# Half 0 of a norm ahead of half 1, attention scores on 64x64 tiles, mLSTM's norm and Hyena's convolution on three engines

## The chip, the cores and the metric

One Trainium2 chip, one of its cores. The metric is the device time of one execution in microseconds. The engines are TensorE (PE, with its weight loads PEld), VectorE (DVE), ScalarE (ACT), GpSimd (POOL) and SyncE (SP), each with its own instruction queue; they wait for each other by semaphores. DMAs are issued from queues of SyncE, Pool and ScalarE.

## The reference

Two transformer blocks on x of 1 x 1024 tokens x 1024 channels, all in float32. The first has a gated linear recurrence (HGRN2) beside a windowed attention; the second has four mixers of 256 channels each beside one another. Both end with a gated FFN of 2816 hidden channels. The parts that the change touches:

```python
def rms_norm(x, g): ...                    # x * rsqrt(mean(x*x) + eps) * g, ahead of each block's projections and FFN, and last
def neighborhood_attention(u, rpb):        # 4 heads of 64, rows of 64 tokens, 8 rows of keys for each row of queries
    s = jnp.einsum('bhrqd,bhrkud->bhrqku', qb, kb) * scale + bias
    p = jax.nn.softmax(s.reshape(s.shape[:4] + (kh * NA_KSPAN,)), axis=-1)
    return jnp.einsum('bhrqku,bhrkud->bhrqd', p, vb)
def mlstm_mixer(u, i_bias, f_bias, norm_g):
    h = rms_norm(h_fwd + h_bwd, norm_g.reshape(ML_HEADS, 1, ML_HEAD_DIM))
    return (jax.nn.sigmoid(o) * h).astype(u.dtype)
def hyena_mixer(u, conv_w, conv_b, ...):   # a depthwise convolution of 3 taps over 768 channels, then two long convolutions
    uc = depthwise_conv(u, conv_w, conv_b)
...
y = jnp.concatenate([y_ssd, y_na, y_ml, y_hy], axis=-1) @ w_out[l]
x = x + g1 * y
h = rms_norm(x) * (1 + sc2) + sh2
x = x + g2 * ((jax.nn.silu(h @ ffn_w_gate[l]) * (h @ ffn_w_up[l])) @ ffn_w_down[l])
```

## The kernel before

x lies in SBUF channels-first: 8 tiles of 128 channels, each with 1024 tokens, which are two halves of 512. The large products are made in float32r with both operands split in a rounded part and a remainder, three passes for each (L615 to L617, L2091 to L2093): ScalarE rounds the raw weights (L626, L2105), VectorE subtracts (L650, L2152).

The kernel is a list of stages. At the end of one, TensorE, ScalarE and VectorE each add one to `stage_done` and wait for the other two (L3803); SyncE and Pool don't, they wait on single semaphores. A `woven` stage has a main part and a second one, the fill, from which each engine takes some steps at places fixed by `yield` counts. So the projections of block 2 and the filters' transform fill the mixers' stages.

**Merges and FFN.** `linear_split` (merge_out of block 1, merge_2 of block 2) makes the output projection in 4 weight groups of 4 fills; a fill is one tile of one half, 24 matmuls, in the order tile 0 half 0, tile 0 half 1, tile 1 half 0, and so on. VectorE evacuates a fill into x (L1939, L3712). `ffn` runs 33 steps, "G" (gate and up, 4 fills) and "D" (down, 16 fills of 6 matmuls) with 6 banks; the last step is a D, evacuated by L2174. `Squares` goes along with the last D step and with the merges: ScalarE squares each fresh piece of x (L491), VectorE adds it to the sum of its half (L499), two fills later.

**The norm.** `SplitNorm` stands at the start of `ffn` and of the projections. TensorE multiplies the two sums by a matrix of ones (L522), ScalarE takes Ln of both (L529) and Exp of both (L532), each with its table; for each half VectorE scales 8 tiles (L548), ScalarE shifts and rounds them (L538), VectorE makes the remainder (L552). Ahead of it in an FFN, ScalarE and VectorE split the first weights (L2105, L2152); in the projections, three groups of weights (L2496, L2504). `first()` in `ffn` (L2059 to L2064) follows this tile by tile. In ffn_1 Pool stores x tile by tile to DRAM (`x_kept`, L2047) during the last step, since the projections' norm scales x in place. `norm` makes the last norm, with its scaling at L991 and four stores.

**Attention.** `neighbourhood` treats 16 rows of queries in 32 items, a row and a pair of heads. Pool clears QD (L2873, L2874) and writes q of two heads on the diagonal of a 128x128 tile of it (L2880), so that one product of 128 by 128 with 512 keys (L2904) gives the scores of both heads. Each engine goes through the items in one order: TensorE scores(i), turn(i-2), values(i-3) and a fill step; VectorE score plus bias with its maximum (L2946) and the scaling of item i-1 (L2953); ScalarE Exp (L2961), the copy of turned probabilities (L2968), the outputs (L2976). Two banks hold scores.

**mLSTM's norm and Hyena's convolution.** Another woven stage. Its main part is `ml_norm` (L3321 squares, L3322 sums, L3334 root, L3325 to L3330 scaling, gain, output gate) and then the transposes `to_fm` (L2645, L2634). Its fill is `Hyena.conv_*`: for each of 6 tiles of 1024 tokens VectorE makes three taps (`convolve`, L2291 to L2293), TensorE transposes (L3473), ScalarE copies (L3483). Two tiles are made between the squares' sum and the root's use, four after the scaling. The next stage is the transform on TensorE (L3514).

Of the kernel before, what the change touches and what calls it, by code (L numbers as in the profile page):

```python
# [472 lines left out]
class Squares:  # L473

    def __init__(self, pg):
        m = Mem(pg.big, M_H, M_PARTS)  # L480
        self.sums, self.buf = m(2, HALF), m(2, HALF)
        self.x = pg.x
        self.squared, self.added = pg.shared_sem("norm_squares", 2 * KT), pg.shared_sem("norm_added", 2 * KT - 2)

    def square(self, e, i):

        tile, s = divmod(i, 2)
        if i >= 4:
            self.added.wait(e, i - 3)
        dst = self.sums[:, s, :] if i < 2 else self.buf[:, s, :]  # L490
        e.activation(dst, self.x[:, tile, s * HALF:(s + 1) * HALF], ACT.Square).then_inc(self.squared.sem, 1)  # L491

    def add(self, e, i):

        s = i % 2
        self.squared.wait(e, i + 1)
        if i >= 4:
            self.added.wait(e, i - 3)
        e.tensor_tensor(self.sums[:, s, :], self.sums[:, s, :], self.buf[:, s, :], ALU.add).then_inc(self.added.sem, 1)  # L499


class SplitNorm:
# [5 lines left out]
    def __init__(self, pg, scale, shift, high, low, y, rs=None, kept=None):  # L508
        self.pg, self.scale, self.shift, self.high, self.low, self.y, self.kept = pg, scale, shift, high, low, y, kept
        self.squares = pg.squares  # L510
        self.rs = pg.squares.sums if rs is None else rs
        self.ms, self.rt = pg.shared_sem("norm_sums", 2), pg.shared_sem("norm_roots", 2)
# [6 lines left out]
    def sums(self, e):  # L519

        for s in range(2):
            e.matmul(self.pg.ps[:, s, :], self.pg.ones, self.squares.sums[:, s, :], start=True, stop=True).then_inc(self.ms.sem, 1)  # L522

    def roots(self, e):

        rs = self.rs
        for s in range(2):
            self.ms.wait(e, s + 1)
            last = e.activation(rs[:, s, :], self.pg.ps[:, s, :], ACT.Ln, bias=self.pg.eps[:, 0:1], scale=1.0 / D)  # L529
        self.pg.achain(e)(last)  # L530
        for s in range(2):
            e.activation(rs[:, s, :], rs[:, s, :], ACT.Exp, scale=-0.5).then_inc(self.rt.sem, 1)  # L532
# [8 lines left out]
    def take_low(self, e, s):  # L541

        if self.kept is not None and s == 0:
            e.wait_ge(self.kept, 16 * KT)
# [11 lines left out]
def linear_split(pg, name, w, evac, act=None, first=None):  # L556
# [14 lines left out]
    pg.squares = squares = Squares(pg)  # L571
# [14 lines left out]
    def tensor(e):  # L586
        for g in range(NG):
# [17 lines left out]
            for q in range(2 if g == 0 and act is not None else 0, fills):  # L605
                t, s = divmod(q, 2)
                f = f0 + fills * g + q
                pg.bank_free(e, f)
# [11 lines left out]
    def scalar(e):  # L620
# [17 lines left out]
        for g in range(NG):  # L638
            if g + 2 < NG:
                weights(g + 2)  # L640
            for q in range(fills):
                i = fills * g + q
                e.wait_ge(pg.ps_free, f0 + i + 1)
                squares.square(e, i)

    def vector(e):
# [19 lines left out]
        for g in range(NG):  # L666
            for q in range(fills):
                t, s = divmod(q, 2)
# [7 lines left out]
        for i in range(NG * fills - 2, NG * fills):  # L676
            squares.add(e, i)
# [266 lines left out]
def norm(pg, name, src, dst, spans, scale, shift, aux=None, squares=None, sync=None):  # L944

    n = len(spans)  # L950
    sq, ms = pg.shared_sem("norm_squares", 0 if squares else KT * n), pg.shared_sem("norm_sums", n)
    rt, md = pg.shared_sem("norm_roots", n), pg.shared_sem("norm_scaled", KT * n)
    rs = pg.scratch(n, HALF)

    def scalar(e):
        ch = pg.achain(e)
        if aux is not None:
            aux(e)
        for s, w in enumerate(spans if squares is None else []):
            for k in range(KT):  # L960
                e.activation(dst(s)[:, k, :], src(s)[:, k, :], ACT.Square).then_inc(sq.sem, 1)
        for s, w in enumerate(spans):
            ms.wait(e, s + 1)
            last = e.activation(rs[:, s, 0:w], pg.ps[:, s, 0:w], ACT.Ln, bias=pg.eps[:, 0:1], scale=1.0 / D)
        ch(last)
        for s, w in enumerate(spans):
# [3018 lines left out]
```

## Time and profile before

| | us |
|---|---|
| three runs | 3731.52, 3742.67, 3749.08 |
| median | 3742.67 |
| the profiled execution | 3744.54 |
| its span, first to last instruction | 3742.9 |

| engine | busy us | share |
|---|---|---|
| TensorE | 3433.6 | 92% |
| VectorE | 1750.2 | 47% |
| ScalarE | 974.2 | 26% |
| Pool | 153.8 | 4% |

The mean granted TensorE clock is 0.944 of full speed. Busy times are sums over the whole span; what a stage is worth is read from its own stretch of the timeline. A product in float32 shows as two records (passes), and a record's duration is longer than the distance to the next, since records overlap. In a row of the timeline "x2" after the shape says that two instructions were merged into one row, whose time is from the first's start to the last's end; in brackets stands how long the engine was idle before it and what released it.

### The profile page before, as it was taken

How to read it: one execution, taken by the hardware profiler on the slowest of the kernel's cores; microseconds unless marked ns; L12 is line 12 of the kernel's file. 1: busy time of each engine (PE TensorE's matmuls, PEld its weight loads, DVE VectorE, ACT ScalarE, POOL GpSimd, SP SyncE). 2: the span in 40 equal slices, each digit the busy share in tenths (PEclk: the TensorE clock that was granted, in tenths of full speed). 3: DMA queues.
4: the chain of work that ended last, by engine and by line, in shares of the span. 5: the costliest groups of instructions: out<-in, count | busy, mean ns of one | idle time of the engine just before them, and what ended most of it. 6: DMA issues, size and time to landing. Idle time of an engine off the chain costs nothing. (4 is left out here: it accounts for less than half of the span.)

```text
span 3742.9 us, 39802 instructions
## 1 busy us (share of the span) xinstructions
PE 3433.6 (92%) x15608; PEld 2582.2 (69%) x15608; DVE 1750.2 (47%) x2949; ACT 974.2 (26%) x1612; POOL 153.8 (4%) x272
## 2 busy tenths in 40 slices
PE   7999988887999999999997988897787999999997
PEld 4476544445787788888886876674465778888886
DVE  5547445445133444444447543453846344343335
ACT  2326522222322321111113232532211231111112
POOL 3100000000100000000000011010000000000000
PEclk8999998895999999999998999998798999999998
DMA  5430000001433132222222132133223111111111
GB/s 215 164 124 12 20 23 12 23 1 37 144 96 129 51 102 80 88 78 78 88 69 93 42 94 86 51 120 111 89 90 140 40 57 50 51 45 45 56 45 45
DMA packets 75771, 279.51 MB, mean 75 GB/s; under 512 B 10583, under 2 KB 30039, under 8 KB 58104
## 3 DMA queue, kind: packets, MB, share of 16 engines
q1 hardware_dynamic: 37048, 166.63, 13.1%
q0 software_dynamic: 21936, 102.66, 7.6%
q10 hardware_dynamic: 16656, 8.42, 1.3%
q8 instruction: 88, 1.44, 0.2%
q14 instruction: 43, 0.35, 0.0%
HBM read 246.11 MB, written 31.59 MB: 74 GB/s over the span
## 5 line engine op out<-in xcount | busy, mean ns | idle before, releaser
L2091 PE MATMUL banks<-input_parts,weight_parts 128*128 128x512 f32 x1344 | 522.8, 389 | 0.0
L2092 PE MATMUL banks<-input_parts,weight_parts 128*128 128x512 f32 x1344 | 522.8, 389 | 0.0
L2093 PE MATMUL banks<-input_parts,weight_parts 128*128 128x512 f32 x1344 | 522.8, 389 | 0.0
L2165 DVE TENSOR_TENSOR before_split<-before_split,banks 128x512 f32<-128x512 f32 x88 | 60.6, 688 | 557.1 <-PE banks L2093 556.9
L2174 DVE SCALAR_TENSOR_TENSOR x<-banks,parameters,x 128x512 f32<-128x512 f32 x352 | 254.8, 748 | 113.7 <-PE banks L2093 113.2
L2093 PEld LDWEIGHTS banks<-input_parts,weight_parts 128*128 128x128 f32 x1344 | 252.3, 188 | 52.4
L2091 PEld LDWEIGHTS banks<-input_parts,weight_parts 128*128 128x128 f32 x1344 | 252.3, 188 | 52.4
L2092 PEld LDWEIGHTS banks<-input_parts,weight_parts 128*128 128x128 f32 x1344 | 252.3, 188 | 52.4
L2091 PE MATMUL banks<-hidden_parts,weight_parts 128*128 128x512 f32 x704 | 273.9, 389 | 0.0
L2092 PE MATMUL banks<-hidden_parts,weight_parts 128*128 128x512 f32 x704 | 273.9, 389 | 0.0
L2093 PE MATMUL banks<-hidden_parts,weight_parts 128*128 128x512 f32 x704 | 273.9, 389 | 0.0
L1531 PE MATMUL banks<-work,weight_ring 128*128 128x512 f32 (+1 forms) x640 | 268.9, 582 | 0.5 <-ACTq L3803 0.5
L1531 PEld LDWEIGHTS banks<-work,weight_ring 128*128 128x128 f32 x640 | 128.0, 203 | 132.8 <-issue 127.4
L2105 ACT ACTIVATE weight_parts<-weight_ring 128x2048 fp32r<-128x2048 f32 x66 | 125.8, 1906 | 335.1 <-PE banks L2093 333.5
L2152 DVE TENSOR_TENSOR weight_parts<-weight_ring,weight_parts 128x2048 fp32r<-128x2048 f32 x66 | 151.3, 2292 | 74.7 <-ACT weight_parts L2105 74.7
L2119 ACT ACTIVATE hidden_parts<-before_split 128x512 fp32r<-128x512 f32 x88 | 55.6, 632 | 477.1 <-DVE before_split L2165 477.1
L1713 DVE SCALAR_TENSOR_TENSOR x<-x,work,banks 128x128 f32<-128x128 f32 x320 | 111.3, 348 | 139.6 <-PE banks L1557 129.1
L2093 PEld LDWEIGHTS banks<-hidden_parts,weight_parts 128*128 128x128 f32 x704 | 132.1, 188 | 27.5
L2092 PEld LDWEIGHTS banks<-hidden_parts,weight_parts 128*128 128x128 f32 x704 | 132.1, 188 | 27.4
L2091 PEld LDWEIGHTS banks<-hidden_parts,weight_parts 128*128 128x128 f32 x704 | 132.1, 188 | 27.4
L2477 PE MATMUL banks<-mix_high,ring_parts 128*128 128x512 f32 x320 | 135.6, 424 | 12.1 <-DVEq L3803 4.2
L2478 PE MATMUL banks<-mix_low,ring_parts 128*128 128x512 f32 x320 | 130.3, 407 | 0.0
(540 smaller groups left out, 5698.3 us busy)
## 6 DMA issues: line engine op xcount, KB each, us to landing
weight_ring<-in_w_gu SPq DMA_DIRECT2D x44, 1024.0 KB, 4.8
weight_ring<-in_mod_w POOLq DMA_DIRECT2D x24, 1024.0 KB, 5.3
weight_ring<-in_w_down SPq DMA_DIRECT2D x22, 1024.0 KB, 4.8
weight_ring<-in_w_merge SPq DMA_DIRECT2D x24, 512.0 KB, 3.7
weight_ring<-in_dft SPq DMA_DIRECT2D x12, 1024.0 KB, 5.0
x<-in_x_t POOLq DMA_DIRECT2D x2, 4096.0 KB, 18.9
weight_ring<-in_w_ada_rest POOLq DMA_DIRECT2D x8, 1024.0 KB, 5.3
weight_ring<-in_w_hgrn SPq DMA_DIRECT2D x8, 1024.0 KB, 4.9
```

The source lines that it names most:

```text
L1531: mm = e.matmul(pg.ps[:, bank_of(h, n), 0:b - a], slot[:, (2 * k + t) * P:(2 * k + t + 1) * P], h1[:, k, a:b], start=(k == 0), stop=(k == ...
L1713: ins = e.scalar_tensor_tensor(out=S[:, 8 * d + (q + 1) % 8, :], in0=S[:, 8 * d + q % 8, :], scalar=dec[:, d, 4 * t + c:4 * t + c + 1], in ...
L2091: e.matmul(bank, w_hi, hi, start=(k == 0), stop=False)
L2092: e.matmul(bank, w_hi, lo, start=False, stop=False)
L2093: mm = e.matmul(bank, w_lo, hi, start=False, stop=(k == len(terms) - 1))
L2105: e.activation(SH[:, n % 2, :], pg.slots[g % 2][:, 0:2048], ACT.Copy).then_inc(high.sem, 1)
L2119: e.activation(FH[:, t % 4, half(s)], F[:, t % 2, half(s)], ACT.Copy).then_inc(hid_high.sem, 1)
L2152: e.tensor_tensor(SL[:, n % 2, :], pg.slots[g % 2][:, 0:2048], plain(SH[:, n % 2, :]), ALU.subtract).then_inc(split.sem, 1)
L2165: e.tensor_tensor(a, a, pg.ps[:, (ff + 1 - f0) % NB, :], ALU.mult).then_inc(pg.ps_free, 2)
L2174: e.scalar_tensor_tensor(out=x[:, tile, half(s)], in0=pg.ps[:, (ff - f0) % NB, :], scalar=gate(tile), in1=x[:, tile, half(s)], op0=ALU.mul ...
L2477: e.matmul(bank, w_hi[:, c], MH[:, k, t], start=start, stop=False)
L2478: e.matmul(bank, w_hi[:, c], ML[:, k, t], start=False, stop=False)
```

## The change

- `Squares` gets the order of the pieces, keeps one rotating pair of buffers for both halves, and in `linear_split` adds a piece directly after its evacuation. `Roots` holds the ones-product, Ln and Exp of one half.
- In `linear_split` the last group goes tile 0 and 1 of half 0, then of half 1. Ahead of its last fill TensorE makes half 0's ones-product into a free bank, and ScalarE its Ln and Exp before the last square. ScalarE rounds and VectorE splits the next FFN's first weights before the last two squares.
- In `ffn` the last D step makes all 8 tiles of half 0 first; the ones-product and the root of half 0 are placed before its fill 12. The stages after it take only half 1's sum and root, after the rounding of half 0. `norm_last` replaces `norm`.
- x is stored to `x_kept` in 16 pieces with a semaphore for each half.
- Attention: q is loaded as it is, with one DMA. For each row of queries four products of 64x64 by 512 keys are issued together; an item is now a row and two heads that lie on different partitions (the weights' columns, gains and bias tables are reordered on the host to match). QD and its memsets go.
- mLSTM's norm: ScalarE squares. The gain is multiplied into the sigmoid of the output gate by Pool, once, after it has issued the filter loads.
- Hyena's convolution: ScalarE makes the middle taps of all six tiles ahead of the root, VectorE the outer taps of tiles 0 to 4, Pool those of tile 5. The order of the transposes is 0, 1, 2, 3, 5, 4.
- Some semaphores are shared between stages; this changes no wait.

```diff
@@ Squares
     def square(self, e, i):
-        tile, s = divmod(i, 2)
-        if i >= 4:
-            self.added.wait(e, i - 3)
-        dst = self.sums[:, s, :] if i < 2 else self.buf[:, s, :]
+        (tile, s), a = self.order[i], self.adds_below(i)
+        if i in self.first:
+            dst = self.sums[:, s, :]
+        else:
+            dst = self.buf[:, a % 2, :]
+            if a >= 2:
+                self.added.wait(e, a - 1)
         e.activation(dst, self.x[:, tile, s * HALF:(s + 1) * HALF], ACT.Square).then_inc(self.squared.sem, 1)
+class Roots:
...
+    def sum(self, e, s, bank):
+        self.squares.summed(e, s)
+        e.matmul(bank, self.pg.ones, self.squares.sums[:, s, :], start=True, stop=True).then_inc(self.ms.sem, 1)
+    def root(self, e, s, bank):
+        v = self.rs[:, s, :]
+        self.ms.wait(e, s + 1)
+        self.pg.achain(e)(e.activation(v, bank, ACT.Ln, bias=self.pg.eps[:, 0:1], scale=1.0 / D))
+        e.activation(v, v, ACT.Exp, scale=-0.5).then_inc(self.rt.sem, 1)
@@ linear_split
+    half_of = lambda g, q: divmod(q, 2) if g < NG - 1 else divmod(q, 2)[::-1]
...
+                if f == f0 + NG * fills - 1:
+                    pg.bank_free(e, f + 1)
+                    squares.roots.sum(e, 0, early)
...
+                if i == NG * fills - 2:
+                    e.wait_ge(pg.ps_full, f0 + fills * (NG - 1))
+                    squares.weights_high(e)
+                if i == NG * fills - 1:
+                    squares.roots.root(e, 0, early)
                 e.wait_ge(pg.ps_free, f0 + i + 1)
                 squares.square(e, i)
...
-                if fills * g + q >= 4:
-                    squares.add(e, fills * g + q - 2)
+                squares.add(e, fills * g + q)
+                if fills * g + q == NG * fills - 2:
+                    squares.weights_low(e)
@@ ffn
+    pg.squares = squares = Squares(pg, [(i % KT, i // KT) for i in range(2 * KT)])
...
+                if n == NS - 1 and q == 12:
+                    e.wait_ge(pg.ps_free, ff - 1)
+                    squares.roots.sum(e, 0, early)
...
+                    if q == 12:
+                        squares.roots.root(e, 0, early)
...
-        take_high(0, 0)
+        norm.take_high(e, 0)
         norm.roots(e)
-        norm.take_high(e, 0)
         norm.take_high(e, 1)
@@ neighbourhood
-        e.memset(QD[0:64, :, :, 64:128], 0.0)
-        e.memset(QD[64:128, :, :, 0:64], 0.0).then_inc(tables.sem, 1)
...
+        e.dma_start(qf, proj.nqk[0:2].rearrange("t p n -> p t n")).then_inc(moved.sem, 16)
...
+        def scores(row):
+            _, _, base = where(2 * row)
+            if row:
+                sm.wait(e, 2 * row)
+            for n in range(2):
+                for w in range(2):
+                    rows = slice(64 * w, 64 * w + 64)
+                    mm = e.matmul(pg.ps[64 * n:64 * n + 64, w, :], qf[rows, n, row * 64:row * 64 + 64],
+                                  kf[rows, n, base * 64:base * 64 + HALF], start=True, stop=True)
+                    if n == 1:
+                        mm.then_inc(sc.sem, 1)
@@ mlstm
-        ch(e.tensor_tensor(SQ, flat, flat, ALU.mult))
+        squares.wait(e, 1)
...
-            ch(e.tensor_tensor(tokens, tokens, pg.param("ml_g")[:, a * P:(a + 1) * P].unsqueeze(1).to_broadcast([P, NCH, P]), ALU.mult))
+            if a == 0:
+                e.wait_ge(gains, 1)
...
+    def gate_gains(e):
+        e.wait_ge(pg.stage_done, 3 * (k_at + 1))
+        e.tensor_tensor(OG, OG, pg.param("ml_g").unsqueeze(1).to_broadcast([P, NCH, 256]), ALU.mult).then_inc(gains, 1)
@@ Hyena
+        self.tap_order, self.turn_order, self.on_pool = [0, 5, 1, 2, 3, 4], [0, 1, 2, 3, 5, 4], [5]
...
+        for n, (tap, at) in enumerate(((t, 0), (12 + t, 2))):
+            e.tensor_scalar(self.product, U[:, at:at + T], pg.col("hcw", tap), None, ALU.mult).then_inc(done, 1)
+            e.wait_ge(done, 2 * n + 3)
+            e.tensor_tensor(out, out, self.product, ALU.add).then_inc(done, 1)
+            e.wait_ge(done, 2 * n + 4)
...
+        for t in self.tap_order:
+            e.activation(self.XC[:, t, :], self.U[:, t, 1:T + 1], ACT.Identity, bias=pg.col("hcb", t),
+                         scale=pg.col("hcw", 6 + t)).then_inc(self.middle_tap, 1)
```

## Rows read from the trace of the kernel before

**Rows 1.** The page's first part: engine, busy us (share), instructions.
```profile
PE 3433.6 (92%) x15608; PEld 2582.2 (69%) x15608; DVE 1750.2 (47%) x2949; ACT 974.2 (26%) x1612; POOL 153.8 (4%) x272
```

**Rows 2.** Timeline, merge_2 to ffn_2: start us, us, engine, line, what.
```profile
2987.16 0.75 DVE L3712 SCALAR_TENSOR_TENSOR x<-banks,parameters,x 128x512 f32<-128x512 f32 x1 [4.09 <-PE banks L617]
...
2989.27 0.69 DVE L499 TENSOR_TENSOR work<-work 128x512 f32<-128x512 f32 x1 [0.15 <-ACT work L491]
2990.04 1.91 ACT L2105 ACTIVATE weight_parts<-weight_ring 128x2048 fp32r<-128x2048 f32 x1 [0.81 <-DVEq L3803]
...
2991.97 1.28 ACT L529 ACT_TABLE_LOAD   x1
...
2996.50 2.74 DVE L548 SCALAR_TENSOR_TENSOR input_plain<-x,parameters,work 128x512 f32<-128x512 f32 x4 [2.16 <-ACT work L532]
...
2998.16 0.77 PE L2059 MATMUL banks<-input_parts,weight_parts 128*128 128x512 f32 x1 [6.11 <-ACT input_parts L538]
```

**Rows 3.** Timeline, merge_out to ffn_1; window in ffn_2 (busy us PE, PEld, DVE..., clock, DMA).
```profile
1281.01 0.75 DVE L1939 SCALAR_TENSOR_TENSOR x<-banks,parameters,x 128x512 f32<-128x512 f32 x1 [4.09 <-PE banks L617]
...
1292.00 0.77 PE L2059 MATMUL banks<-input_parts,weight_parts 128*128 128x512 f32 x1 [5.55 <-ACT input_parts L538]
...
2999.00:3002.00 3.00, 3.00 (x8) 2.32 (x8) 3.00 (x6) 3.00 (x6) 0.00 (x0) 0.50 0.00 0
```

**Rows 4.** Timeline, ffn_1 to projections, and from ffn_2's last evacuation to the output's scaling.
```profile
2024.89 1.06 ACT L2496 ACTIVATE ring_parts<-weight_ring 128x1024 fp32r<-128x1024 f32 x1 [1.24 <-DMA weight_ring<-in_w_xbc]
...
2025.97 1.23 DVE L2504 TENSOR_TENSOR ring_parts<-weight_ring,ring_parts 128x1024 fp32r<-128x1024 f32 x1 [1.07 <-ACT ring_parts L2496]
...
2030.57 2.74 DVE L548 SCALAR_TENSOR_TENSOR x<-x,parameters,work 128x512 f32<-128x512 f32 x4 [3.37 <-ACT work L532]
...
3718.41 0.75 DVE L2174 SCALAR_TENSOR_TENSOR x<-banks,parameters,x 128x512 f32<-128x512 f32 x1
...
3727.12 10.69 DVE L991 SCALAR_TENSOR_TENSOR work<-x,parameters,work 128x512 f32<-128x512 f32 x16 [5.91 <-ACT work L967]
```

**Rows 5.** Start of the attention stage: timeline and windows (last: clock, DMA share, GB/s).
```profile
2328.14 1.83 POOL L2873 MEMSET work<- 64x2048 f32 x1
...
2338.00:2340.00 2.00, 2.00 (x11) 1.65 (x10) 0.00 (x0) 0.78 (x2) 1.32 (x3) 1.00 1.04 209
...
2342.00:2344.00 2.00, 0.00 (x0) 0.00 (x0) 0.00 (x0) 0.00 (x0) 0.00 (x0) 1.00 1.00 399
...
2352.17 2.05 PE L2904 MATMUL banks<-work 128*128 128x512 f32 x2 [10.28 <-DMA work<-na_values]
```

**Rows 6.** Timeline of the attention stage, one of its 32 items to the next.
```profile
2365.69 1.02 PE L2904 MATMUL banks<-work 128*128 128x512 f32 x2
...
2368.58 1.02 PE L2904 MATMUL banks<-work 128*128 128x512 f32 x2
...
2369.63 0.69 DVE L2946 CUSTOM_DVE_ANT_0 work<-banks,work 128x512 f32<-128x512 f32 x1 [1.40 <-PE banks L2904]
```

**Rows 7.** Timeline of block 1's attention: products on halves of the array.
```profile
360.83 1.08 PE L1371 MATMUL banks<-x,work 128*64 128x256 f32 x8
...
362.54 1.13 PE L1346 MATMUL banks<-work 64*128 64x512 f32 x4
```

**Rows 8.** Timeline, the stage of mLSTM's norm and Hyena's convolution.
```profile
2685.35 2.29 DVE L3321 TENSOR_TENSOR work<-work 128x2048 f32<-128x2048 f32 x1
...
2704.62 0.81 DVE L2291 TENSOR_SCALAR work<-work,parameters 128x1024 f32<-128x1024 f32 x1
...
2716.89 1.28 DVE L2293 SCALAR_TENSOR_TENSOR work<-work,parameters 128x1024 f32<-128x1024 f32 x1
...
2720.25 0.60 ACT L3483 ACTIVATE work<-banks 128x512 f32<-128x512 f32 x1 [0.26 <-PE banks L3473]
```

**Rows 9.** L2735 alone (duration ns min/median/max, first and last start); timeline of Pool.
```profile
L2735 DVE TENSOR_TENSOR work<-work x14: 424/426/841, 2190.2 to 2207.2; 128x256 f32<-128x256 f32 x14
...
2189.55 5.56 POOL L2762 TENSOR_TENSOR work<-work,parameters 128x256 f32<-128x256 f32 x8
```

More of the change, by code:

```diff
@@ L519, in sums @@
     def sums(self, e):
-        for s in range(2):
-            e.matmul(self.pg.ps[:, s, :], self.pg.ones, self.squares.sums[:, s, :], start=True, stop=True).then_inc(self.ms.sem, 1)
+        self.of_half.sum(e, 1, self.pg.ps[:, 5, :])
     def roots(self, e):
[L526 to L532, printed above, removed]
+        self.of_half.root(e, 1, self.pg.ps[:, 5, :])
     def take_high(self, e, s):
@@ L570, in linear_split @@
     parts = lambda g: [slice(0, 2048)] if g else [slice(0, 1024), slice(1024, 2048)]
-    pg.squares = squares = Squares(pg)
+    half_of = lambda g, q: divmod(q, 2) if g < NG - 1 else divmod(q, 2)[::-1]
+    place = [half_of(g, q) for g in range(NG) for q in range(fills)]
+    pg.squares = squares = Squares(pg, [(2 * (i // fills) + t, s) for i, (t, s) in enumerate(place)])
+    early = pg.ps[:, (f0 + NG * fills) % 8, :]
     def sync(e):
@@ new lines, in norm_last, with vector @@
+def norm_last(pg, name, src, dst, gain, squares, sync):
+    of_half = Roots(pg, squares, pg.scratch(2, HALF))
+    scaled = pg.shared_sem("norm_scaled", 2 * KT)
+    bank = pg.ps[:, 1, :]
+    def vector(e):
+        for s in range(2):
+            of_half.rt.wait(e, s + 1)
+            for k in range(KT):
+                e.scalar_tensor_tensor(out=dst(s)[:, k, :], in0=src(s)[:, k, :], scalar=gain(k), in1=of_half.rs[:, s, :],
+                                       op0=ALU.mult, op1=ALU.mult).then_inc(scaled.sem, 1)
+    pg.stage(name=name, sync=lambda e: sync(e, scaled), tensor=lambda e: of_half.sum(e, 1, bank),
+             scalar=lambda e: of_half.root(e, 1, bank), vector=vector)
@@ L2044, in pool @@
         load(FT + 1, 0, False)
-        for k in range(KT if spill else 0):
-            e.wait_ge(pg.ps_free, first_fill[NS - 1] + 2 * k + 2)
-            e.dma_start(spill[0][:, k, :], x[:, k, :]).then_inc(spill[1], 16)
+        for i in range(2 * KT if spill else 0):
+            tile, s = squares.order[i]
+            e.wait_ge(pg.ps_free, first_fill[NS - 1] + i + 1)
+            e.dma_start(spill[0][:, tile, half(s)], x[:, tile, half(s)]).then_inc(spill[1][s], 16)
     def tensor(e):
@@ L2896, in tensor @@
         yield 20
[L2897 to L2905 removed]
+        moved.wait(e, 16 * 6)
+        def scores(row):
[9 more added lines that the diff above has]
+                        mm.then_inc(sc.sem, 1)
         def turn(i):
@@ L2937, in vector @@
         yield 20
-        moved.wait(e, 16 * 9)
+        moved.wait(e, 16 * 6)
         for i in range(N + 3):
```

219 lines of the change are left out of this document (108 added, 111 removed).

## The prediction

> **What bounds the kernel now.** I read the page first: TensorE is busy 92% of the span [rows 1], so only a stretch in which it stands still, or a matmul that goes away, can shorten the kernel. Then the timeline at each place that the diff touches. Four seams come first, where a stage must sum the squares of x, take roots and scale before the next matmul. At merge_2 to ffn_2 the last evacuation starts at 2987.16 and the first product at 2998.16, 11.0 us later [rows 2]; merge_out to ffn_1 is the same, 1281.01 to 1292.00 [rows 3]. In between stand in series: the last add (to 2989.96), the rounding of the next weights (1.91), a table load, two Ln, a second table load, two Exp, the first scale [rows 2]. After such a pause the granted clock is 0.50, 1.2 GHz, for some 3 us [rows 3]. Next the attention stage: TensorE idles 10.28 us for operands and then needs 2.89 us for each of 32 pairs, VectorE waiting for its scores [rows 5, 6]. Last, the stage of mLSTM's norm and Hyena's convolution, which VectorE fills from 2685.35 to its end; TensorE waits for it [rows 8].
>
> **The change part by part.**
>
> *Seams at the merges (two).* The last weight group is done half 0 first, so Ln and Exp of half 0 (2991.97 to 2996.50 is 4.5 with both halves' Ln, some 3.9 with one [rows 2]) run on ScalarE while TensorE does the last fill, which lasts 5.4 us (VectorE's idle of 4.09, its evacuation and add [rows 2]); the next weights are rounded (1.91 and 2.29) under the last two fills. One ones-product (two passes of 0.43, as two take with their tail 1.02 in [rows 6]: 0.85) moves from the seam into TensorE's own line: +0.85. What is late next: the last evacuation, one square, one add, now without the add of the fill before: 2.3 us to the barrier instead of 2.8. Then VectorE scales at once, and the first product follows 1.66 us later (2996.50 to 2998.16 [rows 2]). So 11.0 becomes 0.85+2.3+1.66 = 4.8: 6.2 us each. Half 1's second pair of table loads runs from the eighth rounding on (6.1+4.0 = 10.1 us after VectorE starts) and is wanted when VectorE has done 16 steps of 0.66, after 10.6: hidden with 0.5 to spare; if not, the same cost moves there. TensorE now pauses some 4 us, broken by a product, instead of 11. In [rows 3] eight passes ran in 3.0 us at 0.50, which at full clock are worth 1.8: between 0 and 1.8 per seam comes back, I take 0.9. Squares are now waited for directly after each evacuation; in the first two groups that leaves VectorE behind for about 12 us, under a group of 21.8 us of matmuls, with eight banks. Nothing. Two merges: **14.2**.
>
> *Seam ffn_1 to projections.* Here the rounding of three weight groups, started after the barrier and paced by their DMAs, ends at 2025.97+1.23 = 2027.20, and only then Ln and Exp, until scaling starts at 2030.57 [rows 4]. With half 0's root ready, 3.37 goes; the moved product (+0.85) and 0.25 of tail (below) come back: **2.3**. The spill of x by halves makes 16 issues on Pool, one each 1.36 us of fill, Pool is otherwise idle; half 0 lands long before.
>
> *End of ffn_2.* 3718.41 to 3727.12 is 8.71 [rows 4]. Root 0 is placed before the last four fills; ScalarE stands 3.9 us in it, and four squares are late. VectorE catches up behind the last fill with two evacuations and adds; I count 0.25 longer than now. Afterwards 0.85+3.3 = 4.2 from the old last evacuation to the first scale: **4.4**. Root 1 (4.9 after the barrier) meets VectorE's ninth scale at 5.3.
>
> *Attention, start.* Two memsets (1.83 each) ahead of Pool's issues go; the four DMAs that wrote q in 64-word pieces become one: in that stretch the 16 DMA engines are full at 209 GB/s, beside 399 for the others [rows 5], so 1 MB takes 5.0 us and would take 2.6. All else moves up: 3.6+2.3 = 5.9. The pause falls to 4 us; the half clock after it (two passes in 2.05 at 2352.17 [rows 5], 1.02 later [rows 6]) may go: 0 to 2.3, I take 1.2. **7.1**.
>
> *Attention, scores.* Now a row's two pairs cost two products of two passes of 0.43, 1.71 us, half of it on zeros. After, four products of 64x64 on four quadrants. No row shows four at once. Nearest: two row halves, four passes of 512 columns, span 1.13 [rows 7] where one after the other is 1.71; two column halves, eight passes of 256 columns in 1.08 for 1.71 [rows 7]. Both directions run two at a time, so I take four at a time: 0.85 and 0.11 for the change of shape (the first pass lasts longer). Then TensorE needs 1.71−0.96 = 0.75 us less per row, 12.0 in 16 rows. But now the scores come for a whole row at once and TensorE waits for the row's second maximum, and VectorE, which now idles 1.40 of each 2.88 [rows 6], must take the second pair behind the first. Following two iterations through the three queues, a row can wait up to 0.4: between 5.5 and 12, I take **9**. If only two run at a time, nothing, and 16 changes of shape cost 2; if one at a time, 4×0.85 instead of 1.71, +27.
>
> The Trainium skill ("TensorEngine Tiling (Array Packing)", Key Properties) says that independent tiles work in parallel, and that changing the mode drains TensorE. By the first the sum stays at 41.0; by the second alone it loses what a drain takes, which no row here shows apart.
>
> *mLSTM norm and convolution.* VectorE loses the squares (2.29 [rows 8], but it waits for ScalarE's instead, 1.91 for as many columns [rows 2]: −0.3), two gain products (1.23 each for 1024 columns [rows 4]), five middle taps (0.81 each) and a whole tile (0.81+1.28+1.28 [rows 8] with gaps). Its sum from 2685.35: 4.4 to the reduction, two tiles of 2.53, 0.35+2.33+2.5, three tiles, 22.2. ScalarE does six middle taps ahead of the root (six of 1.06 [rows 4], then a table load and the root, 1.6): root at 10.1, wanted at 9.5, +0.6. Alone this is 22.9, but the transposes and copies behind it, half a tile in 0.86 (0.60 and 0.26 [rows 8]), end at 27.4; now the last copy ends at 2720.85, after 35.5. That would be 8.1. Against it stands Pool's tile. Beside eight products of 256 columns on Pool, VectorE's 0.42 steps take 0.84 [rows 9], so 256 columns on Pool cost VectorE 0.41. Pool's tile has two sums and two scalings of 1024: two sums 3.3, the scalings (no row) between 1.8 and 4.2: 5 to 8.5 longer on VectorE, all before its last tile. Then VectorE ends at 28 to 31, plus the 2.7 from the last tap's end, 2718.17, to the last copy's [rows 8]: the stage takes 31 to 34. I take 31.5: **4.0**, with 1.4 and 8.1 as ends. The gate times gain on Pool (2048 columns) falls after the filter loads, when VectorE waits for TensorE: nothing.
>
> The Trainium skill ("SBUF — State Buffer", SBUF: two separate sides) states that the port pair of VectorE and GpSimd is a lock held for a whole instruction. The doubled row agrees in direction; by it, VectorE would stand through whole Pool operations, and the sum would be 38.4, with 1.4 for 4.0: that is rival (b).
>
> **Sum.** 14.2+2.3+4.4+7.1+9+4.0 = 41.0. The profiled execution took 3744.54, span 3742.9; 3744.5−41.0 = 3703.5. The median of the runs is 1.9 lower, so I say **3702**.
>
> **Rivals.**
> (a) *Two at a time or bound by the chain:* the new shape of the scores gives nothing. For it: four quadrants are shown nowhere. Against: both halves of the shape are. +9 to +11: 3712.
> (b) *Pool takes it back:* contention at its upper end or a Pool scaling far slower than its sum, so that tile 5 is what the last transposes wait for, and the half clocks stay. +3+3: 3708; it shares the range of the forecast.
> (c) *One quadrant at a time at full cost:* TensorE runs the four in turn: 3702+9+27 = 3738, about no change.
> (d) *Slower than before:* as (c), and each pass must leave the array before the next enters. A pass then takes its full 0.59 to 0.69 and not 0.43; eight of 0.69 are 5.5 per row, for 1.71: +61 against 32 gained elsewhere, 3772. It decides from 3.7 us per row on. Against it: the pass of one half starts within the other's in [rows 7].
> (e) *Seams not shortened:* root 1 late, or something else gates the first product at both merges; the 12.4 and half clocks stay: 3716. For: 0.5 us of margin only. Against: the chain of [rows 2] has no other member.
>
> **How the numbers follow.** Forecast with (b) 0.72, (a) 0.12, (e) 0.05, (c) 0.05, (d) 0.02, others 0.04. Range: the forecast's own is 3703−11 (12 for 9, 8.1 for 4.0, clocks in full) to +8, 3691 to 3711; the runs before differ by 17 us among themselves, so with (a) and (e) 3690 to 3722. A measurement can tell about 0.5%, 19 us: below 3724 is faster. Forecast, (a), (e) and 0.01 of the others are faster: 0.90; (c) and 0.02 within: 0.07; (d) and 0.01 slower: 0.03.
>
> **What would show it.** In the profile after: the first product of ffn_1 and ffn_2 some 4 us after the last evacuation starts; Ln, Exp inside the last fills; scaling of the output within 3.5 us of the last evacuation; TensorE's wait ahead of the first scores near 4 us; scores' passes starting four together and a row's period near 5.2 us; VectorE's taps at about 2 us instead of 1.28 beside Pool. Wrong if the passes of the scores start one after the other, if a wait stands ahead of half 1's scaling, or if the last copy of the convolution waits for Pool's tile.

## The result, and the profile after

Six runs of the kernel after took 3701.46 to 3722.32 us, median 3711.8; six of the kernel before, 3731.52 to 3749.08, median 3744.11. The ratio is 0.991 (95% interval 0.9897 to 0.9924): 32 us or 0.9% faster. A second set gave 3712.55 and 0.9917 (0.9896 to 0.9939). The profiled execution took 3702.47, its span is 3700.5.

The forecast for the profiled execution was 3703.5. It hit for a wrong reason: TensorE was 12.6 us ahead before the first changed line, and the change gave 30 us where 41 were counted. A landmark tells the two apart, the first product of merge_out; nothing ahead of it is changed.

| | landmark | span | from landmark to end |
|---|---|---|---|
| before, profile of [rows 1 to 9] | 1191.22 | 3742.9 | 2551.7 |
| before, second profile | 1194.37 | 3747.0 | 2552.6 |
| after | 1178.59 | 3700.5 | 2521.9 |
| after, second profile | 1185.71 | 3708.5 | 2522.8 |

The first pair and the second both give 29.8 us, 2.5 less than the medians, whose interval is some 5 wide to either side. Page and seams of after, answering [rows 1], [rows 3] (timeline of merge_out to ffn_1, two windows behind it) and [rows 2] (merge_2 to ffn_2):

```profile
PE 3408.2 (92%) x15672; PEld 2560.3 (69%) x15672; DVE 1743.0 (47%) x2938; ACT 993.2 (27%) x1627; POOL 168.4 (5%) x282
...
1269.34 0.75 DVE L1938 SCALAR_TENSOR_TENSOR x<-banks,parameters,x 128x512 f32<-128x512 f32 x1 [2.00 <-PE banks L650]
...
1271.68 2.74 DVE L575 SCALAR_TENSOR_TENSOR input_plain<-x,parameters,work 128x512 f32<-128x512 f32 x4 [0.20 <-DVEq L3870]
...
1273.40 0.76 PE L2074 MATMUL banks<-input_parts,weight_parts 128*128 128x512 f32 x1 [0.68 <-ACT input_parts L565]
...
1274.00:1278.00 4.00, 4.00 (x11) 0.50 0.99 413
1280.00:1282.00 2.00, 2.00 (x11) 1.00 0.00 0
```

```profile
2956.47 0.75 DVE L3777 SCALAR_TENSOR_TENSOR x<-banks,parameters,x 128x512 f32<-128x512 f32 x1 [2.00 <-PE banks L650]
...
2958.82 2.74 DVE L575 SCALAR_TENSOR_TENSOR input_plain<-x,parameters,work 128x512 f32<-128x512 f32 x4 [0.21 <-DVEq L3870]
...
2960.81 0.77 PE L2074 MATMUL banks<-input_parts,weight_parts 128*128 128x512 f32 x1
```

VectorE scales 2.35 us after its last evacuation starts (9.34 before), and the product follows at 4.06 and 4.34 (10.99). Behind the first seam the granted clock was 0.50 (1.2 GHz): eleven passes fall in the 4 us of the window, some begun or ended outside it.

The last step of ffn_1 and the start of the projections, and the end of ffn_2, answering [rows 4]:

```profile
1996.34 0.74 DVE L2193 SCALAR_TENSOR_TENSOR x<-banks,parameters,x 128x512 f32<-128x512 f32 x1
...
2010.95 1.23 DVE L2522 TENSOR_TENSOR ring_parts<-weight_ring,ring_parts 128x1024 fp32r<-128x1024 f32 x1 [1.18 <-ACT ring_parts L2514]
2012.09 2.07 DVE L575 SCALAR_TENSOR_TENSOR x<-x,parameters,work 128x512 f32<-128x512 f32 x3
...
3680.33 0.39 PE L2111 MATMUL banks<-hidden_parts,weight_parts 128*128 128x512 f32 x1
...
3681.60 0.74 DVE L2193 SCALAR_TENSOR_TENSOR x<-banks,parameters,x 128x512 f32<-128x512 f32 x1
...
3684.74 1.42 DVE L992 SCALAR_TENSOR_TENSOR work<-x,parameters,work 128x512 f32<-128x512 f32 x2 [0.21 <-DVEq L3870]
```

Scaling starts where the third weight group's remainder ends, as planned. At the end of ffn_2 the last product starts at 3680.33, but the evacuation only at 3681.60: VectorE stands behind squares that ScalarE makes after half 0's root.

The attention's start and one row of it, answering [rows 5, 6]:

```profile
2328.51 1.99 PE L2921 MATMUL banks<-work 64*64 64x512 f32 x8 [4.31 <-DMA work<-na_values]
...
2372.89 1.09 PE L2921 MATMUL banks<-work 64*64 64x512 f32 x8
2373.91 0.66 PE L2931 MATMUL banks<-parameters,work 128*128 128x128 f32 x4
...
2374.96 0.72 ACT L2980 ACTIVATE work<-work 128x512 f32<-128x512 f32 x1 [2.17 <-DVE work L2967]
...
2376.00 0.60 PE L2931 MATMUL banks<-parameters,work 128*128 128x128 f32 x4
...
2376.29 0.44 ACT L2995 ACTIVATE work<-banks 64x64 f32<-64x64 f32 x2
...
2376.87 1.13 PE L2941 MATMUL banks<-work 128*128 128x128 f32 x8 [0.28 <-ACT work L2995]
...
2378.63 1.09 PE L2921 MATMUL banks<-work 64*64 64x512 f32 x8
```

Eight passes on four quadrants span 1.09 us, the next step starts 1.02 after the first: they do run four at a time (one after the other eight passes of 0.43 are 3.4), where the two pairs of a row took 1.71. But this row still takes 5.74 us (2372.89 to 2378.63), 5.69 in the mean of rows 2 to 15, for 5.77 before. TensorE stands ahead of the values at 2376.87, until ScalarE has copied the outputs of two items earlier (2376.29). The product that made them ended at 2372.26; the copy stands in ScalarE's queue behind the exponential of the new row (2374.96), for whose maximum ScalarE waited 2.17 us.

The stage of norm and convolution, answering [rows 8, 9]:

```profile
2659.45 1.91 ACT L3353 ACTIVATE work<-work 128x2048 f32<-128x2048 f32 x1 [15.24 <-DVEq L3870]
...
2663.81 1.28 DVE L3485 SCALAR_TENSOR_TENSOR work<-work,parameters 128x1024 f32<-128x1024 f32 x1
2663.81 3.92 POOL L3513 TENSOR_SCALAR work<-work,parameters 128x1024 f32<-128x1024 f32 x1 [4.20 <-ACT work L3540]
2665.13 1.94 DVE L3486 SCALAR_TENSOR_TENSOR work<-work,parameters 128x1024 f32<-128x1024 f32 x1
2666.99 1.27 DVE L3485 SCALAR_TENSOR_TENSOR work<-work,parameters 128x1024 f32<-128x1024 f32 x1
...
2667.82 2.65 POOL L3515 TENSOR_TENSOR work<-work 128x1024 f32<-128x1024 f32 x1
...
2668.30 3.25 DVE L3486 SCALAR_TENSOR_TENSOR work<-work,parameters 128x1024 f32<-128x1024 f32 x1
...
2670.57 3.70 POOL L3513 TENSOR_SCALAR work<-work,parameters 128x1024 f32<-128x1024 f32 x1
...
2671.85 2.83 DVE L3345 TENSOR_TENSOR work<-work 128x2048 f32<-128x2048 f32 x1
...
2674.35 2.53 POOL L3515 TENSOR_TENSOR work<-work 128x1024 f32<-128x1024 f32 x1
...
2674.71 4.50 DVE L3350 TENSOR_TENSOR work<-work 128x1024 f32<-128x1024 f32 x2
...
2690.71 0.48 PE L3577 MATMUL banks<-work,weight_ring 128*128 128x256 f32 x1 [0.72 <-ACTq L3870]
```

From the squares to the transform's first product it takes 31.3 us, 35.6 before (2685.35 to 2720.93). Pool is done at 2676.88, VectorE at 2687.06: nothing waits for Pool's tile, but VectorE's steps beside Pool are longer (1.94, 3.25, 2.83, 4.50).

### The profile page after: what moved, and what is told of

It reads as the page before. It is cut to its first block and busy times, and to the rows that moved or that the text cites. A ratio compares the mean times of both kernels' runs of the same rounds, so it can differ in the third digit from the quotient of the medians.

```text
span 3700.5 us, 39966 instructions
## 1 busy us (share of the span) xinstructions
PE 3408.2 (92%) x15672; PEld 2560.3 (69%) x15672; DVE 1743.0 (47%) x2938; ACT 993.2 (27%) x1627; POOL 168.4 (5%) x282
## 5 line engine op out<-in xcount | busy, mean ns | idle before, releaser
L2109 PEld LDWEIGHTS banks<-hidden_parts,weight_parts 128*128 128x128 f32 x704 | 132.2, 188 | 27.9 <-issue 0.5
L2110 PEld LDWEIGHTS banks<-hidden_parts,weight_parts 128*128 128x128 f32 x704 | 132.2, 188 | 27.9 <-issue 0.5
L2135 ACT ACTIVATE before_split<-banks 128x512 f32<-128x512 f32 x88 | 52.7, 599 | 289.2 <-PE banks L2111 289.2
```

The lines of the kernel that those rows point to most:

```text
L2109: e.matmul(bank, w_hi, hi, start=(k == 0), stop=False)
L2110: e.matmul(bank, w_hi, lo, start=False, stop=False)
L2135: e.activation(F[:, t % 2, half(s)], pg.ps[:, (ff - f0) % NB, :], ACT.Silu).then_inc(silu.sem, 1)
```

## Experiments

Each kernel changes after and nothing else, unless said otherwise. Whole times move with the clock by more than these edits are worth, so each is read from its own stretch.

**1. Is the lead of 11.7 us the change's?** The kernel before, profiled again.

> The kernel before, unchanged, profiled a second time. In the profiled pair TensorE of after was already 11.7 us ahead when the last evacuation of merge_out started (1269.34 for 1281.01), ahead of every line that the change touches. Theory: that is the granted clock of one execution and not the change, so in this second profile the same evacuation starts anywhere between 1269 and 1281, and the stretches of half clock in block 1 lie elsewhere or are shorter. Rival: the change moves something in block 1 (a semaphore, a place in memory); then the evacuation starts at 1281 again, within 1 us. From there to the first product of ffn_1 both expect 11.0 us.

It took 3748.72, and the evacuation came at 1283.04. That lies outside both expectations, 2 us from the rival's 1281, so alone it settles nothing. The kernels below decide. Block 1 up to merge_out is the same in all, yet their landmarks were 1178.03, 1178.32, 1188.53, 1189.03, 1191.89, 1194.33 and 1195.79. Where the time goes is seen in two windows of unchanged code, in the kernel of experiment 2 and then in after (window, its length, PE busy, clock, DMA share, GB/s):

```profile
550.00:560.00 10.00, 10.00 (x78) 0.50 0.00 0
560.00:570.00 10.00, 10.00 (x75) 0.50 0.01 2
```

```profile
550.00:560.00 10.00, 7.77 (x94) 1.00 0.01 2
560.00:570.00 10.00, 8.19 (x54) 1.00 0.01 2
```

The same stage ran at 1.2 GHz in one execution and at 2.4 in the other. The first pair differs elsewhere: of its 12.6 us 8.0 had come by 113 us, where before was at 0.50 from 85 to 100 us and after at 1.00 from 84.8 to 91.6. Kernels with the change lie on both sides of before's 1191.22 and 1194.37, so a lead of this size needs no change, as the theory has it; that the change moves block 1 by a us or two these profiles can't rule out. After, profiled again:

> The kernel after, unchanged, in a second set of runs and with a second profile, beside which the next kernel is read. Theory (the 12.6 us by which the profiled after was ahead of the profiled before at the barrier ahead of merge_out came from the clock in one execution): here that barrier can lie anywhere from 1176 to 1193 (1176.07 and 1188.71 in the first pair, 1191.85 and 1193.27 in others), while the rest, from that barrier to the last one, takes 2519 us again, within 4, as in the first profile (2519.4), and 2549 in before. Ratio to before 0.991 to 0.993. Rival (the change itself moves the first part): the barrier lies at 1176 again, within 1.

Median 3712.55, profiled run 3710.46. The barrier ahead of merge_out came at 1183.19, from it to the last barrier 2520.3 us passed (2519.4 in the first profile, 2549.15 in before). The rival (1176 again, within 1) is out.

**2. What Pool's tile is worth.** Tile 5's outer taps on VectorE.

```
-        self.tap_order, self.turn_order, self.on_pool = [0, 5, 1, 2, 3, 4], [0, 1, 2, 3, 5, 4], [5]
+        self.tap_order, self.turn_order, self.on_pool = [0, 1, 2, 3, 4, 5], [0, 1, 2, 3, 4, 5], []
...
-        for t in range(5):
+        for t in range(6):
```

> After, with the outer taps of the convolution's tile 5 made by VectorE and not by Pool. ScalarE's squares and middle taps and Pool's gate factors stay. Theory (VectorE loses more beside Pool than Pool does for it): in after Pool works from 2663.81 to 2676.88, and VectorE's steps beside it take 1.94 and 3.25 for 1.28, 2.83 for 2.33 and 4.50 for 2.50, 5.1 us too much together; two taps of 1.28 come back to VectorE, 2.6. So the stage from ScalarE's squares to the first product of the transform, 31.3 us in after (2659.45 to 2690.71), takes 28.8, and the kernel gains 2.5 us. Rival (the prediction's first sizes: the tile is worth its VectorE time): the stage takes 31.3+2.6 = 33.9, and the kernel loses 2.6.

Median 3708.43, ratio 0.9887 (0.9864 to 0.9909). The stage takes 27.9 us, with every step back at its length:

```profile
2671.98 1.91 ACT L3353 ACTIVATE work<-work 128x2048 f32<-128x2048 f32 x1 [16.84 <-DVEq L3870]
...
2682.74 2.29 DVE L3345 TENSOR_TENSOR work<-work 128x2048 f32<-128x2048 f32 x1
...
2685.06 2.48 DVE L3350 TENSOR_TENSOR work<-work 128x1024 f32<-128x1024 f32 x2
...
2699.92 1.35 PE L3577 MATMUL banks<-work,weight_ring 128*128 128x256 f32 x5 [0.73 <-ACTq L3870]
```

The theory holds, by 3.3 us instead of 2.5: the tile on Pool costs 0.66+1.97+0.54+2.02 = 5.2 on VectorE and saves 2.6 there. Of the 2.6 that this leaves, 0.9 goes into a wait for ScalarE's root, so VectorE ends 1.7 earlier; the transposes and copies behind its last step end another 1.6 earlier, for they start behind the gate product, which ended 19.8 us into the stage in after and 15.6 here. Without Pool's tile the stage gains 7.7 us on before (35.6 to 27.9): the steps that ScalarE took over and the gain product that left VectorE. No run parts these two.

**3. What eats the shorter scores.** ScalarE copies outputs at the head of its iteration.

```
         for i in range(N + 4):
+            if i >= 4:
+                q = i - 4
+                pv.wait(e, q + 1)
...
+                ins.then_inc(yo.sem, 1)
             if i < N:
                 sm.wait(e, i + 1)
...
-            if i >= 4:
...
-                ins.then_inc(yo.sem, 1)
```

> After, with ScalarE's copies of an item's outputs made ahead of its exponentials instead of behind the copy of turned probabilities; nothing else is moved. In after a row of the attention takes 5.74 us, and TensorE stands 0.42 of them between the second turn and its values (2376.45 to 2376.87), until the copies of the outputs two items earlier are made (2376.29 to 2376.73). Theory (that wait is what eats the shorter scores): with it gone a row takes 5.3 to 5.45, 16 rows 4.5 to 7 us less. Rival (the loop of scores, maximum, exponential, copy and values as a whole sets the row, and the wait only shows where it is spent): the row stays within 0.1 of 5.74 and TensorE waits at another place. Second rival (the copies now delay the exponentials): the row takes 5.9 or more.

Median 3705.94, ratio 0.9895 (0.9878 to 0.9911). A row takes 5.34 us:

```profile
2373.52 1.09 PE L2921 MATMUL banks<-work 64*64 64x512 f32 x8
2374.54 0.66 PE L2931 MATMUL banks<-parameters,work 128*128 128x128 f32 x4
...
2376.62 0.60 PE L2931 MATMUL banks<-parameters,work 128*128 128x128 f32 x4
...
2377.07 1.16 PE L2941 MATMUL banks<-work 128*128 128x128 f32 x8
...
2378.86 1.09 PE L2921 MATMUL banks<-work 64*64 64x512 f32 x8
```

The wait ahead of the values is gone (0.45 from turn to values, 0.87 in after) and no other took its place; the mean of rows 2 to 15 is 5.34 too. The first scores of the stage came 2.2 us later than in after, its end 2.3 us earlier: 4.5 us, the lower end of the theory. From barrier to barrier this profile took 2523.0 us, 3.6 more than after: the mLSTM stage behind it took 227.5 us for 221.1, with 60 us at 0.50 for 44. That stage varied by 9 us between the profiles.

**4. Does the clock follow TensorE's pauses?** Products that nobody reads.

```
@@ linear_split, behind the last fill
+        pg.bank_free(e, f0 + NG * fills + 1)
+        for n in range(10):
+            e.matmul(pg.ps[:, (f0 + NG * fills + 1) % 8, :], SH[:, (NG - 1) % 2, 0:P], HH[:, 0, half(0)], start=True, stop=True)
@@ ffn, and sixteen alike ahead of moved.wait in neighbourhood
         norm.sums(e)
+        for n in range(4):
+            e.matmul(pg.ps[:, 4, 0:P], pg.ones, pg.ones, start=True, stop=True)
```

> After, with products that nobody reads put where TensorE stands still: ten of 128x512 behind the last fill of both merges and four small ones behind half 1's ones-product in both FFNs, and sixteen small ones ahead of the wait for the attention's operands. Nothing is left out. In after the first products behind the seam of merge_out ran at half clock from 1273.40 to 1279.3 (granted 0.50), fourteen passes of 0.425 for 0.225, which is 2.8 us lost; behind merge_2 1.3 us; at the attention's start from 2328.51 to 2335.1, some 2.5 us. Theory (the clock falls because TensorE stands still): granted 1.00 throughout these stretches, 2.8+1.3+2.5 = 6.6 us less in all, if the added products don't delay the barrier (ten passes of 0.23 in a pause of 2.9 us). Rival (the clock falls by itself at such places, whatever TensorE does): the half clocks stay, and the time is that of after or up to 1 us more.

Median 3706.37, ratio 0.9897 (0.9881 to 0.9914). Seam merge_out to ffn_1, a window behind it, and the attention's start:

```profile
1268.88 2.43 PE L654 MATMUL banks<-input_parts,weight_parts 128*128 128x512 f32 x10
1269.08 0.75 DVE L1941 SCALAR_TENSOR_TENSOR x<-banks,parameters,x 128x512 f32<-128x512 f32 x1 [2.00 <-PE banks L650]
...
1273.31 0.48 PE L2077 MATMUL banks<-input_parts,weight_parts 128*128 128x512 f32 x1
...
1274.00:1278.00 4.00, 4.00 (x20) 1.00 1.01 416
...
2324.58 3.73 PE L2918 MATMUL banks<-parameters 128*128 128x128 f32 x32
2331.14 1.13 PE L2928 MATMUL banks<-work 64*64 64x512 f32 x4 [2.83 <-DMA work<-na_values]
```

At both merges the granted clock stayed at 1.00: 2.6 us won behind the first, 0.6 behind the second (1.4 us at half clock lose 0.7, so 1.3 was sized too high). At the attention's start the small products were used up 2.83 us before the operands came, and the clock was 0.50 again at 2332 to 2336. So theory at two places of three; at the third the pause was longer than the filling. Experiments 7 and 8 fill it, with 24 and 22 small products: there the clock was 1.00 at all three places, and the first eight passes of the scores took 1.09 us for 1.99. The 3.2 us don't show in this profile's total: from barrier to barrier it took 2521.6 us, 2.2 more than after, since the three stages from the projections to the attention took 5.7 longer.

**5. The end of the FFNs.** Half 0's ones-product and root one fill earlier, the product in bank 6.

```
-                if n == NS - 1 and q == 12:
-                    e.wait_ge(pg.ps_free, ff - 1)
+                if n == NS - 1 and q == 11:
...
-                    if q == 12:
+                    if q == 11:
                         squares.roots.root(e, 0, early)
```

> After, with half 0's ones-product and root in the last step of both FFNs one fill earlier: ahead of fill 11 instead of 12, into bank 6. In after half 0's Exp ends at 3680.43 in the last step of ffn_2, and the four squares behind it hold back VectorE, whose last evacuation starts at 3681.60 and last add ends at 3684.53, while the last product ends at 3680.7. Theory (ScalarE's late root is what makes the end of ffn_2 worth 3.8 us and the one of ffn_1 1.1, where 4.4 and 2.3 were predicted): the last evacuation starts 0.6 to 0.8 us after the last product's start less its length as everywhere else, the last add ends 1.2 us earlier, at both places, 2.4 us in all; TensorE may wait up to 0.2 for the seventh sum of half 0. Rival (VectorE's own line, sixteen evacuations and fourteen adds, is what is late): the last add stays where it is, and ahead of fill 11 TensorE waits for the sum: 0 to 1 us more.

Median 3710.33, ratio 0.9923 (0.9906 to 0.9939).

```profile
3690.85 0.39 PE L2110 MATMUL banks<-hidden_parts,weight_parts 128*128 128x512 f32 x1
3691.27 0.75 DVE L2192 SCALAR_TENSOR_TENSOR x<-banks,parameters,x 128x512 f32<-128x512 f32 x1
...
3694.36 2.05 PE L526 MATMUL banks<-work,parameters 128*128 128x512 f32 x2 [3.13 <-DVEq L3870]
3694.42 2.74 DVE L992 SCALAR_TENSOR_TENSOR work<-x,parameters,work 128x512 f32<-128x512 f32 x4 [0.21 <-DVEq L3870]
```

The evacuation follows the last product by 0.42 instead of 1.27, and the scaling by 3.57 instead of 4.41: 0.8 us won, not 1.2, so the root did hold VectorE back. But ahead of fill 11 TensorE now stood some 0.4 us for the seventh sum, where 0.2 was allowed. The ones-product of half 1 then ran at half clock (2.05 for 1.10 in after), the second root came later and VectorE waited 0.6 for it; nothing was left. Whether it pays in the mean these runs can't tell.

**6. The projections' start.** Half 0 is scaled ahead of the weights.

```
+        norm_2.scale_half(e, 0)
         proj.lows(e, 0)
-        norm_2.take_low(e, 0)
+        norm_2.take_low(e, 0, scale=False)
```

> After, with the projections begun in another order: VectorE scales half 0 of x (eight steps) and ScalarE rounds it before the three weight groups are rounded and split; in after the weights come first. In after VectorE stands from 2002.2 until 2006.73 for the weights' DMAs, ends them at 2012.09, and only then scales; the first product is at 2013.74, and its second pass over the remainders of x can begin only behind the eight scalings, at 2017.4. Theory (the order of the weights and not the root sets this seam by now, so that the early root was worth little here): VectorE scales from 2002.2 to 2007.6, the first group is split at 2008.9, the first product follows at about 2009, and the remainders come at 2012.2 instead of 2017.4: 4.5 to 5.2 us less for the kernel. Rival (x of half 0 has not yet been stored when VectorE wants to scale it in place, or the DMAs of the weights are the bound for all that follows): under 1.5 us.

Median 3710.76, ratio 0.993 (0.9911 to 0.9948). Scaling began with the barrier (2011.91), the first product came 14.5 us after the last evacuation instead of 17.4 (16.7 to 17.1 in five further profiles with the old order), and the stage was 2.95 us shorter (barrier to barrier 141.5 for 144.4). That lies between the theory's 4.5 and the rival's "under 1.5": ScalarE rounded eight tiles before the first weights, so these were split only at 2019.03.

**7. All edits together.** Twenty-four small products ahead of the attention instead of 16.

> After with all of the single edits together: taps of tile 5 on VectorE, outputs copied ahead of the exponentials, the root of half 0 one fill earlier, half 0 scaled ahead of the projections' weights, and products that nobody reads in the pauses at both merges (ten and four small ones) and, now twenty-four instead of sixteen, ahead of the attention's operands. Theory (each gain lies on TensorE's line at its own place and they add): 3.3 us of the convolution stage (31.3 to 27.9 in its run), 4.5 of the attention's rows (5.74 to 5.34), 2.4 of the FFNs' ends, 4.7 of the projections' start, 3.9 of half clocks at the merges and up to 2.5 at the attention's start: 19 to 21 us below after, some 3691 for after's 3711.8, a ratio to before of 0.986. Rival (what is gained ahead of a DMA-bound stretch, as the load of mLSTM's operands, is waited for there; or half clocks fall elsewhere): 8 to 12 us.

Median 3697.66, ratio 0.9886 (0.9869 to 0.9904). From the landmark to the end it takes 2503.6 us, 18.3 less than after (from barrier to barrier 2501.4, 18.0 less, where 19 to 21 were expected): the gains add, but for a little. In the whole this profile doesn't show it, since its block 1 was slow (landmark 1194.33).

**8. A version that beats both.** To it come products at the end of both FFNs and at the projections' start, and there VectorE splits the first weights after six scalings; ahead of the attention stand 22 small products.

> The kernel of all single edits with three further ones. At the end of both FFNs twelve and twenty-four products that nobody reads, and twenty small ones behind the projections' first ones-product; at the projections' start VectorE scales six tiles, splits the first weight group and then scales the other two, and ScalarE rounds three tiles ahead of that group; ahead of the attention's operands 22 instead of 24 small products. From the barrier ahead of merge_out to the last one the kernel of all edits took 2501.4 us, after 2519.4. Theory (half clocks and the order of the projections' start are what is left): the first product of the projections comes 2.5 us earlier, half clocks of 4 us behind it and of 1 us at the last ones-product go: 2501.4-2.5-2-1 = 2496, some 23 us below after, a median some 0.6% under that of after in the same set. Rival (the small products delay the first real one, or VectorE waits for the weights' DMA in the middle of its scaling): 2500 to 2504, and about 0.45%.

Median 3696.98 (3691.80 to 3701.16), after in the same set 3712.55 (3704.26 to 3718.58): 15.6 us or 0.4% less, with no overlap; to before 0.9875 (0.9855 to 0.9894). But from barrier to barrier it was 2504.8, past the rival's figure and 3.4 more than in experiment 7, so the further edits gained nothing in sum. The first product came 11.5 us after the last evacuation and at full clock, 2.9 earlier than in experiment 6, and the stage was not shorter (142.4 for 141.5). TensorE's waits in that stage say why (waited for: us in total, times, longest), first in experiment 7, then here:

```profile
PE banks L2492 <- DVE mix_low L585: 0.8, 5, 0.2
```

```profile
PE banks L2497 <- DVE mix_low L585: 3.5, 9, 2.1
```

By these waits VectorE's own line of 32 scalings and remainders and three weight splits bounds this start: a product that starts 2.9 us earlier waits 2.7 longer inside.

## Why the prediction was right, and where it was not

The sign, the range and the order of size held: 3711.8 for 3702. It lies just outside of what the forecast gave itself (3691 to 3711; its ends add up to 10 and not 11), and within 3690 to 3722 because rival (a) was given room. By steps, from the first pair of profiles where no other is named:

| step | predicted | measured |
|---|---|---|
| merges, pause (two) | 12.4 | 11.9 |
| merges, clock (two) | 1.8 | 0.0 |
| ffn_1 to projections | 2.3 | 1.1 |
| end of ffn_2 | 4.4 | 3.9 |
| attention, start | 7.1 | 6.2 |
| attention, scores | 9 | 1.0 |
| norm and convolution | 4.0 | 4.3 |
| not placed, clock among it | 0 | 1.4 |
| sum behind the landmark | 41.0 | 29.8 |

*Merges.* 11.0 became 4.06 and 4.34 plus the 0.85 of the moved ones-product, 4.9 and 5.2 for 4.8: right. Root 1 is never waited for: it was there 10.1 us after VectorE's start and wanted at 10.6, as counted. The clock term was right in kind and uncertain in size: behind merge_out half clock lasted 3.5 us before and 6.1 after, which took 1.3 back, behind merge_2 4.0 and 1.4. In the six profiles of after and of its variants without products in the pause it was 1.4 to 6.1 behind merge_out. In experiments 4, 7 and 8, with products in the pause, there was none at either merge: it is TensorE's standing still there that brings it.

*FFN ends.* The 0.25 for VectorE's catching up was the mis-sized term. Experiment 5: 0.8 of lateness at each end comes from four squares behind the root. At the projections the weights did the rest: in this profile the third group's remainder began 8.9 us behind the barrier, 8.4 before and 8.2 to 8.6 in the other profiles with this order. The second pair gives 1.9 there.

*Attention, start.* Pause 10.28 to 4.31 (4.3 to 6.2 in the other profiles), the 5.9 of memsets and DMA, which no run parts; the first two rows gave another 0.2; the half clock stayed (eight passes in 1.99), so the 1.2 of it was not there. That was this execution's: in the profile of experiment 2, with a pause of 4.33, the first eight took 1.12.

*Attention, scores.* This is the step that failed. The four quadrants were right: TensorE needs 0.69 less per row, 0.75 predicted. What failed is "a row can wait up to 0.4: between 5.5 and 12, I take 9". Two iterations were followed for scores and maxima, and not for the outputs' copies, which free the bank of the values. In ScalarE's queue they stand behind the exponential of the new row, and that one waits for the row's first maximum. TensorE's wait for the copies was 0.42 in the row shown, and without it a row is 0.35 shorter in the mean (experiment 3). What then still misses of the 0.69, 0.26, lies in steps that grew: in experiment 3's row the last fill step takes 0.87 to the scores where one before takes 0.78, and the turn behind the scores 0.05 more, so some 0.14 at the change of shape; the second turn and values take 0.12 more, and why is open. So rival (a), bound by the chain, came true with 0.12; its 3712 is the median, though what bound the row was the order of one queue, and not the chain from scores to exponential as such.

*Convolution.* 31.5 predicted, 31.3 measured, contention 5 to 8.5 predicted, 5.2 measured. That both totals agree so well is luck in part: VectorE ended after 27.7 us, where 28 to 31 were counted, and from there to the last copy it took 3.6 for 2.7. What the prediction didn't draw from its own numbers: 5 on VectorE is more than the 2.6 that the tile spares there.

*Profile and median.* The sum was made against one execution whose block 1 was slow; its neighbour of after had a fast one. The 1.9 between profile and median hid that a single profile is uncertain by some 18 us here (the landmarks).

## What to carry to other kernels

Compare two profiles from a landmark just ahead of the first changed line, not by their spans: what lies before it is the clock's chance. Behind it too a single stage can vary by 9 us, so read a small edit from its own stretch. When a step on the bounding engine shrinks, follow every semaphore that this engine waits for through the other engines' queues for a full period, the one that frees an output bank too, and reorder that queue together with the step. Before a tile goes to Pool, set what it costs VectorE beside it against what it spares VectorE.

## What the runs showed of the hardware

Pool's kinds of operation weigh differently on VectorE. Beside its scaling of 3.92 us three steps of VectorE took 1.28, 1.94 and 1.27, 0.66 too much together. Beside its sums of 2.65 and 2.53 VectorE lost 1.97 and 2.02: a step that started at 2668.30 ended at 2671.55, 1.1 after Pool's sum, as if it had run only behind it; the gate product at 2674.71 also ended 1.1 after Pool's second sum. The lengths were the same, within 0.01, in all six profiles with this tile on Pool. The Trainium skill ("SBUF — State Buffer", SBUF: two separate sides) has the shared ports held for a whole instruction. The sums agree. The scaling does not: it lasted until 2667.73, and under it VectorE's step of 2665.13 was over at 2667.07 and the next one ran in its usual 1.27. The measurement decides.

At the merges the half clock of TensorE is set off by a pause and lasts a varying time: 1.4, 3.1 or 6.1 us behind the same seam of 4.1 us, none with products in the pause. A pause isn't always there: in experiment 2's profile the clock was 0.50 from 546.7 to 584.3, 37.6 us that after ran at 1.00, and in the 14 us before it fell TensorE was busy for 91% of the time, without a gap of 0.5 us. What set that off is open. The Trainium skill ("TensorE: Matmul & The Clock Gate", What's actually happening) says of the slow products at a kernel's start that their number varies from run to run of one kernel; at these seams the traces show the same.
